# Wide output projections, a position-major first down projection, and the norms' folds moved from GpSimd to VectorE in a two-block layer kernel

## What is computed

```python
x = x + merged @ w_out                      # block 1, output projection, 1024 x 1024
h = rmsnorm(x, norm2_g)
up = causal_dwconv(h @ w_up)                # 1024 x 2816
x = x + (gelu(up) * (h @ w_gate)) @ w_down  # 2816 x 1024: the first down projection
h = rmsnorm_2(x, mix_norm_g)                # block 2
proj = h @ w_in                             # 1024 x 3488
...
x = x + y @ w_out_2                         # block 2, output projection
x = x + (silu(h @ w_gate_2) * (h @ w_up_2)) @ w_down_2
```

## Time and profile before

| | |
|---|---|
| median of 3 runs | 797.68 us (797.62 to 798.31) |
| profiled execution, its own time | 797.33 us |
| its span, first to last instruction | 795.5 us |
| around the span | 1.83 us |
| TensorE matmul busy | 787.8 us, 99% |
| VectorE busy | 582.8 us, 73% |
| ScalarE busy | 453.3 us, 57% |
| GpSimd busy | 75.0 us, 9% |
| mean granted TensorE clock | 0.999 |

### The profile page before, as it was taken

How to read it: one execution, slowest core, us unless ns; L and a number is a source line. 1 busy time by engine, 2 the same in 40 slices (tenths; PEclk the granted TensorE clock), 3 DMA queues, 4 the chain that set the end, 5 groups by cost and what they waited for, 6 DMA issues and landing times.

```text
span 795.5 us, 12020 instructions
## 1 busy us (share of the span) xinstructions
PE 787.8 (99%) x4622; PEld 690.9 (87%) x4622; DVE 582.8 (73%) x705; ACT 453.3 (57%) x594; POOL 75.0 (9%) x92
## 2 busy tenths in 40 slices
PE   8999999999999999999999999999999999999997
PEld 8998888888889899999999897888799888888886
DVE  7986897566577898777787877766878766666664
ACT  7679765666345654544454658767455544454444
POOL 2220231000002000000000532410003000000000
PEclk9999999999999999999999999999999999999999
DMA  8645555443545454555454552444345545455521
GB/s 322 243 161 203 183 192 213 158 159 133 184 159 210 156 205 171 178 194 208 163 206 158 183 197 87 156 159 150 139 155 213 196 181 185 184 198 176 206 105 53
DMA packets 21718, 140.88 MB, mean 177 GB/s; under 512 B 3378, under 2 KB 3506, under 8 KB 5682
## 3 DMA queue, kind: packets, MB, share of 16 engines
q1 hardware_dynamic: 21538, 140.13, 48.9%
q10 hardware_dynamic: 144, 0.26, 0.1%
HBM read 139.33 MB, written 1.05 MB: 176 GB/s over the span
## 4 chain that ended last, share of the span: by engine, by line
PE 97%; DVE 1%; ACT 1%; DMA 1%; issue 0%; SPq 0%; DVEq 0%
PE pp L1577 21%; PE pp L1540 20%; PE pp L1542 20%; PE pp L1541 20%; PE pp L1579 10%; PE pp L1695 1%; PE pp L1721 1%; PE pp L1708 1%; DMA first<-in_first 1%; PE pp L1684 1%; DVE wlo L1051 1%; PE pp L1758 0%; PE pp L1630 0%; PE pp L1642 0%; PE pp L1658 0%; PE pp L1650 0%
## 5 line engine op out<-in xcount | busy, mean ns | idle before, releaser
L950 DVE TENSOR_TENSOR wlo<-raw,whi 128x2048 fp32r<-128x2048 f32 x129 | 298.2, 2314 | 96.2 <-ACT whi L525 95.9
L525 ACT ACTIVATE whi<-raw 128x2048 fp32r<-128x2048 f32 x129 | 246.4, 1911 | 101.2 <-PE pp L1542 101.1
L1577 PE MATMUL pp<-ahilo,whi 128*128 128x512 f32 x704 | 221.4, 396 | 0.0
L1540 PE MATMUL pp<-whi,ahi 128*128 128x512 f32 (+2 forms) x412 | 162.8, 395 | 0.0
L1542 PE MATMUL pp<-whi,alo 128*128 128x512 f32 (+2 forms) x412 | 159.4, 387 | 0.0
L1579 PEld LDWEIGHTS pp<-ahilo,wlo 128*128 128x128 f32 x704 | 132.2, 188 | 31.2
L1541 PE MATMUL pp<-wlo,ahi 128*128 128x512 f32 (+2 forms) x412 | 159.2, 386 | 0.0
L1579 PE MATMUL pp<-ahilo,wlo 128*128 128x256 f32 x704 | 138.3, 278 | 0.0
L1540 PE MATMUL pp<-ahi,whi 128*128 128x256 f32 x416 | 118.5, 285 | 1.4 <-DVE wlo L1051 1.4
L1542 PE MATMUL pp<-ahi,wlo 128*128 128x256 f32 x416 | 117.7, 283 | 0.0
L1541 PE MATMUL pp<-alo,whi 128*128 128x256 f32 x416 | 117.7, 283 | 0.0
(11 more groups left out here) (238 smaller groups left out, 780.7 us busy)
## 6 DMA issues: line engine op xcount, KB each, us to landing
raw<-in_slabs SPq DMA_DIRECT2D x125, 1024.0 KB, 4.8
first<-in_first SPq DMA_DIRECT2D x3, 768.0 KB, 6.9
raw<-in_slabs SPq DMA_DIRECT2D x2, 832.0 KB, 4.4
raw<-in_slabs SPq DMA_DIRECT2D x2, 576.0 KB, 3.7
raw<-in_slabs SPq DMA_DIRECT2D x2, 512.0 KB, 9.9
out<-gg SPq DMA_DIRECT2D x3, 256.0 KB, 2.1
xa<-in_final_norm_g SPq DMA_DIRECT2D x1, 512.0 KB, 6.5
first<-in_first SPq DMA_DIRECT2D x1, 480.0 KB, 3.5
```

The lines of the kernel that those rows point to most:

```text
L525: e.activation(whi[slot][:, :], raw[slot][:, :], ACT.Copy).then_inc(hi_ready, 1)
L950: e.tensor_tensor(wlo[slot][:, :], raw[slot][:, :], whi[slot][:, :].bitcast(f32), ALU.subtract).then_inc(lo_ready, 1)
L1540: e.matmul(out, lhs[0], rhs[0], start=first, stop=False, skip_group_check=True)
L1577: e.matmul(out[:, m, :], w[m][0], ACT2[:, k, :], start=k == 0, stop=False, skip_group_check=True)
```

## The change

1. **Output projections wide.** Both use `feature_pairs` on a buffer `ACT0` that holds high and low side by side, into pairs of banks (2 and 3, or 0 and 1, in turn). `residual` becomes two VectorE instructions, one for each half of the pair.
2. **First down projection position-major**, as the second is: 24 matmuls of 512 columns per slab. X is not added in PSUM: at the end ScalarE copies the four banks to SBUF (`rows`), TensorE transposes them back, 16 in all, in two rounds of 8 (`rows_turn`), and VectorE adds the transposed banks to X (`add_rows`). The first round stands inside the last down slab, the second inside block 2's first strip, before its chunk 2.
3. **Folds on VectorE**, in all four norms, at written places of VectorE's program. `sums(2)` takes two tiles for each half instead of one.
4. `WARM` goes from 11 to 10.

```diff
-WARM = 11
+WARM = 10
...
+        elif out_slab(s) is not None:
+            b = ((3, 1) if s < FFN1 else (1, 3))[out_slab(s) % 2]
...
@@ ScalarE, after FFN 1
-            norm_hi(2, pcol[:, MIXG:MIXG + KD], pairs[0][0], range(KD))
-            for i in range(4):
-                squares(2, i)
+            def rows(c, h):
+                e.wait_ge(down_bank, 2 * c + h + 1)
+                e.activation(outp[:, h, 512 * c:512 * c + 512], ps[2 + 2 * h + c][:, :], ACT.Copy).then_inc(rows_out, 1)
+            rows(0, 0)
+            rows(0, 1)
+            norm_hi(2, pcol[:, MIXG:MIXG + KD], pairs[0][0], (0, 1))
+            rows(1, 0)
+            rows(1, 1)
+            norm_hi(2, pcol[:, MIXG:MIXG + KD], pairs[0][0], (2, 3))
             pre(S2_SEQ + 2)
+            squares(2, 0)
+            squares(2, 1)
+            norm_hi(2, pcol[:, MIXG:MIXG + KD], pairs[0][0], range(4, KD))
+            squares(2, 2)
+            squares(2, 3)
...
@@ VectorE
+            def fold(n, i):
+                e.wait_ge(sq_ready, 4 * n + i + 1)
+                ins = e.tensor_tensor(SQ[:, 0:2, :], SQ[:, 0:2, :], SQ[:, 2 * i:2 * i + 2, :], ALU.add)
+                if i == 3 and n in (0, 2):
+                    ins.then_inc(sq_fold, 1)
+                    return
+                link(ins)
+                if i == 3:
+                    e.tensor_tensor(SQ[:, 0, :], SQ[:, 0, :], SQ[:, 1, :], ALU.add).then_inc(sq_fold, 1)
...
                 lo_part(2, cols, raw[2][:, cols], KD - 2, i == 1)
+            for i in range(1, 4):
+                fold(0, i)
             e.wait_ge(pool_small, 1)
...
-                e.scalar_tensor_tensor(X[:, 2 * i:2 * i + 2, :], ps[BANK[g]][:, :].rearrange("p (m n) -> p m n", m=2),
-                                       0.5, X[:, 2 * i:2 * i + 2, :], ALU.mult, ALU.add).then_inc(bank_free["dve"], 1)
+                x = X[:, 2 * i:2 * i + 2, :]
+                link(e.scalar_tensor_tensor(x, out_pair(s)[:, :, 0:SEQ], 0.5, x, ALU.mult, ALU.add))
+                e.scalar_tensor_tensor(x, out_pair(s)[:, :, SEQ:2 * SEQ], 0.5, x, ALU.mult, ALU.add).then_inc(
+                    bank_free["dve"], 1)
...
                     norm_lo(1, pcol[:, G2:G2 + KD], pairs[2][1], pairs[2][0], (2 * i, 2 * i + 1))
+                    if i > 1:
+                        fold(1, i - 1)
...
                 if s == FFN1 - 1:
+                    fold(1, 3)
                     pre(s + 3)
...
-            for b in range(4):
-                e.wait_ge(down_bank, b + 1)
-                e.tensor_tensor(X[:, 2 * b:2 * b + 2, :], ps[2 + b][:, :].rearrange("p (m n) -> p m n", m=2),
+            def add_rows(b):
+                e.wait_ge(rows_T, b + 1)
+                e.tensor_tensor(X[:, 2 * b:2 * b + 2, :], PSX[b][:, :].rearrange("p (m n) -> p m n", m=2),
                                 X[:, 2 * b:2 * b + 2, :], ALU.add).then_inc(x_ready, 1)
-                if b:
-                    norm_lo(2, pcol[:, MIXG:MIXG + KD], pairs[0][1], pairs[0][0], (2 * b - 2, 2 * b - 1))
-            norm_lo(2, pcol[:, MIXG:MIXG + KD], pairs[0][1], pairs[0][0], (6, 7))
-            pre(S2_SEQ + 1)
-            pre(S2_SEQ + 2)
+            for c in range(2):
+                add_rows(2 * c)
+                add_rows(2 * c + 1)
+                norm_lo(2, pcol[:, MIXG:MIXG + KD], pairs[0][1], pairs[0][0], range(4 * c, 4 * c + 4))
+                pre(S2_SEQ + 1 + c)
+            for i in range(1, 4):
+                fold(2, i)
...
@@ TensorE
+            def rows_turn(c):
+                e.wait_ge(rows_out, 2 * c + 2)
+                for m in range(4):
+                    for h in range(HALVES):
+                        o = SEQ * (m % 2) + P * h
+                        ins = e.transpose(PSX[2 * c + m // 2][:, o:o + P],
+                                          outp[:, h, 512 * c + P * m:512 * c + P * m + P], ident[:, :])
+                    if m % 2:
+                        ins.then_inc(rows_T, 1)
...
+                    for a in range(2):
+                        for i in range(4):
+                            if last and which == 1:
+                                c, h, k = a, i // 2, i % 2
...
+                                        weights(slot, k, slice(512 * c, 512 * c + 512), D), first and k == 0, False,
+                                        (lambda: rows_turn(0)) if last and which == 1 and (a, i) == (1, 1) else None)
...
-                    S2_SEQ: lambda k: e.wait_ge(h_lo, 2 * KD + k + 1),
+                    S2_SEQ: lambda k: (rows_turn(1) if k == 2 else None, e.wait_ge(h_lo, 2 * KD + k + 1)),
+                    S2_SEQ + 1: lambda k: e.wait_ge(h_lo, 2 * KD + k + 1),
```

More of the change, by code:

```diff
@@ L106, in half_strip, with out_slab @@
     return None
+def out_slab(s):
+    if S_OUT <= s < FFN1:
+        return s - S_OUT
+    return s - S2_OUT if S2_OUT <= s < FFN2 else None
 def gate_strip(s):
@@ L253, in program @@
         X, T0, T1 = (chunks[:, :, SEQ * i:SEQ * i + SEQ] for i in range(3))
-        ACT2 = sb("ahilo2", [P, KD, 2 * SEQ], f32r)
-        pairs = [(sb("ahi0", [P, KD, SEQ], f32r), sb("alo0", [P, KD, SEQ], f32r)),
+        ACT0, ACT2 = (sb(f"ahilo{i}", [P, KD, 2 * SEQ], f32r) for i in (0, 2))
+        pairs = [(ACT0[:, :, 0:SEQ], ACT0[:, :, SEQ:2 * SEQ]),
                  (sb("ahi1", [P, KD, SEQ], f32r), sb("alo1", [P, KD, SEQ], f32r)),
@@ L347, in program, with out_pair @@
         PSM = (ps[6], ps[7], ps[4], ps[5])
+        def out_pair(s):
+            return pp[((1, 0) if s < FFN1 else (0, 1))[out_slab(s) % 2]]
         def gate_half(c, h):
@@ L369, in program @@
         PSPV2 = ps[5][:, SEQ:2 * SEQ]
+        PSX = (ps[0], ps[1], ps[2], ps[3])
         PSCQ = (ps[3], ps[4], ps[3])
@@ L1419, in _ @@
                     norm_lo(3, pcol[:, FFNG:FFNG + KD], pairs[2][1], pairs[2][0], (2 * i, 2 * i + 1))
+                    if i > 1:
+                        fold(3, i - 1)
                 if s == FFN2 - 1:
+                    fold(3, 3)
                     pre(s + 3)
@@ L1448, in _ @@
         def _(e):
[L1449 to L1459, removed]
-                    e.tensor_tensor(SQ[:, 0, :], SQ[:, 0, :], SQ[:, 1, :], ALU.add).then_inc(sq_fold, 1)
             e.wait_ge(first_in[0], 16)
@@ L1465, in _ @@
             e.tensor_scalar(sp[:, 2, :], pcol[:, LAM:LAM + KD], -1.0, None, ALU.mult).then_inc(pool_small, 1)
-            fold(0)
             for s in range(S_XR, S_G):
@@ L1478, in _ @@
                                 ALU.subtract).then_inc(ya_lo, 1)
-            fold(1)
-            fold(2)
             steps = [0]
@@ L1532, in _, with three @@
                            ropeB[:, 0, h, :], ropeB[:, 1, h, :], 4, 16, mla_ready if i and h else None)
-            fold(3)
         @block.tensor
         def _(e):
-            def three(out, lhs, rhs, first, last):
+            def three(out, lhs, rhs, first, last, between=None):
                 e.matmul(out, lhs[0], rhs[0], start=first, stop=False, skip_group_check=True)
+                if between:
+                    between()
                 e.matmul(out, lhs[0], rhs[1], start=False, stop=False, skip_group_check=True)
@@ L1569, in feature_tiles, with feature_pairs @@
                 return ins
-            def feature_pairs(out, slot, ready):
+            def feature_pairs(out, slot, ready, act=ACT2):
                 for k in range(KD):
@@ L1576, in feature_pairs @@
                     for m in range(2):
-                        e.matmul(out[:, m, :], w[m][0], ACT2[:, k, :], start=k == 0, stop=False, skip_group_check=True)
+                        e.matmul(out[:, m, :], w[m][0], act[:, k, :], start=k == 0, stop=False, skip_group_check=True)
                     for m in range(2):
-                        ins = e.matmul(out[:, m, 0:SEQ], w[m][1], ACT2[:, k, 0:SEQ], start=False, stop=k == KD - 1,
+                        ins = e.matmul(out[:, m, 0:SEQ], w[m][1], act[:, k, 0:SEQ], start=False, stop=k == KD - 1,
                                        skip_group_check=True)
@@ L1611, in sums @@
                     for h in range(HALVES):
-                        ins = e.matmul(sums_bank(n)[:, h:h + 1], SQ[:, 0, P * h:P * h + P], ones[:, 0:1], start=True,
-                                       stop=True, skip_group_check=True)
+                        for i in range(2):
+                            ins = e.matmul(sums_bank(n)[:, h:h + 1], SQ[:, i, P * h:P * h + P], ones[:, 0:1],
+                                           start=(h, i) == (0, 0), stop=(h, i) == (1, 1), skip_group_check=True)
                 else:
@@ L1825, in slab @@
                                         (act[0][:, blk, :], act[1][:, blk, :]), m == 0, True)
+                    elif out_slab(s) is not None:
+                        ins = feature_pairs(out_pair(s), slot, at, ACT0)
                     elif layout == "feature" and kind == "cols":
@@ L1914, in down @@
                     acthi, actlo = act_parts[last]
[L1915 to L1932 removed]
+                    for a in range(2):
```

(13 more changed lines are left out.)

20 lines of the change are left out of this document (2 added, 18 removed).

## The result

The changed kernel takes **793.39 us**, median of 5 runs (793.37 to 793.64), against 797.68 for the kernel before in the same rounds (797.55 to 798.31): a ratio of 0.9948 with an interval of 0.9938 to 0.9959. The profiled execution took 793.6 us, with a span of 791.8.

What follows compares the result with a forecast made beforehand. TensorE, busy for 99% of the span, was taken as the bound. The terms -3.53 - 1.33 + 1.75 + 0.30 - 1.43 + 0.29 = -3.95 us gave 793.4, plus 0.35 for the median: 793.7 us, range 792.8 to 795.4.

Steps and rivals of the forecast that it cites:

- Down projection: First FFN's down projection: eleven slabs go from 5.77 to 5.45 us with 24 wide matmuls instead of 48, -3.53 us.
- Output projections: Both output projections: eight slabs go from 5.76 to 5.57 us, one of them gaining nothing, -1.33 us.
- The transposes: From FFN 1 to block 2: sixteen added transposes cost +1.75 us, and TensorE's wait at the first round +0.30 us.
- narrow place of 0.2 us: Block 2's first strip, chunks 0 and 4: VectorE's work was forecast ready only 0.2 us before TensorE needs it.
- Start: Norm 0's folds leave GpSimd: the 1.43 us wait before slab 2 goes, sums at 20.25 instead of 21.68, -1.43 us.
- the sign that I had named for being wrong: At the start: a first pair whose matmuls start 0.24 us apart would show the forecast wrong.
- Sums 2: Sums of norm 2: four products take 0.92 us where TensorE lost 0.63 before, +0.29 us.
- In the middle of the kernel nothing waited for that: Away from the start, nothing waited for GpSimd's slow additions or the VectorE work they slowed; no gain priced there.
- the gate at the start stays: Rival: GpSimd does not cause VectorE's long instructions, so slab 2 at the start still waits; 795.5 us, chance 0.08.
- block 2's first strip waits: Rival: the path to chunk 4 falls behind by one low part and TensorE waits 2.1 us; 795.8 us, chance 0.10.
- Cost by columns: Rival: matmul cost goes with columns, not the number of matmuls, so wide forms save nothing; 798.6 us, chance 0.02.
- VectorE as the bound in the output projections: Rival: in the eight output slabs the second residual instruction is paid in full, 5.84 us; 799.6 us, chance 0.03.

## Why the prediction was right, step by step

**Down projection**, -3.53 us: right. The pass of 16.59 us was reached, and the split of the second down projection shows that the number of matmuls is the reason.

**Output projections**, 0.19 a slab and none from block 2's slab 0: right. The stretches gave 0.70 and 0.59 for 0.76 and 0.57, and the wait before block 2's slab 1 is there with 0.29 us. Undone, the wide form cost 1.28 in these two stretches.

**The transposes**: right in sum, +1.07 and -2.40 for +1.17 and -2.36, but not by its own step. I had TensorE wait 0.26 us for ScalarE's copies. It didn't: the matmul before started at 434.78 and the transposes at 435.01, the usual 0.23, for ScalarE's copies were done at 433.90 + 1.06 = 434.96. ScalarE's timeline:

```profile
433.90 1.06 ACT L842 ACTIVATE gg<-pp 128x512 f32<-128x512 f32 x2
```

The same time went elsewhere: the last down slab began at 431.25 and block 2 at 437.80, 6.55 us for 5.45 + 0.87 = 6.32. Its first matmul stands 431.56 - 431.25 = 0.31 us before the next, and so does the first one behind the transposes (435.87 to 436.18), where 0.227 is the usual: 0.17 in all. The other 22 are 0.230 apart, 0.07 in all. The one behind the transposes was in the forecast, the one at the slab's start was not. The forecast had the slab's input there "with 0.1 to spare". VectorE made it until 430.42 + 0.69 = 431.11, but TensorE loads it as weights ahead of the matmul: that load started at 431.22, 0.23 us after the load before had ended, where the down slab that starts at 409.22 has its load at 409.11 without a gap. I read this as a short wait for VectorE, which is not shown: the profile names no releaser. Eight transposes cost 435.87 - 435.01 = 0.86 and 441.33 - 440.54 = 0.79 us, as priced. Neither narrow place of 0.2 us opened: behind the last down slab the matmuls follow each other without a gap.

**Start**, -1.43 us: right, but only for an execution whose first matmuls are fast. All three stretched instructions and the 1.43 us wait fell with GpSimd's additions. Counted from the moment at which ScalarE takes up the input, the start went from 15.21 to 13.77 us, 1.44 less. The path was as forecast too: VectorE's second half is ready 10.87 us after that moment (16.99 + 1.22 - 7.34), which from 7.15 makes 18.02 for my 18.0. Two things were missing. The moment itself differs from execution to execution, by 0.3 us in the profiles, and the kernel before's profile had caught an early one; that is 0.19 of the 0.34 by which the profiled 1.09 falls short. And I took the first pair as free of the warm-ups, but in the profiled execution its first four matmuls were 0.24 us apart, the sign that I had named for being wrong. So TensorE reached the sums at 20.59, after the folds' end at 20.27; that is the other 0.16. The medians of both kernels give 1.23 and 1.24, over executions of both sorts.

**Sums 2**: four products for two, 0.92 us forecast and 453.13 - 452.32 = 0.81 measured, and no wait for the folds (they end at 449.37). With the distance ahead of them it makes 453.13 - 452.10 - 0.23 = 0.80 for 0.63 before: +0.17 for the +0.29 of the sum.

**"In the middle of the kernel nothing waited for that"**: true of the kernel before, not of this one. With wide slabs GpSimd's last additions come 0.22 us late at sums 1 and 3. The number was not hurt, as the change moves them, but I had priced at nothing what is worth 0.66 us together with the wide slabs.

**The rivals.** That the gate at the start stays fell with both kernels that move norm 0's folds. That block 2's first strip waits fell with the 15.33 us stretch. Cost by columns fell with the split. VectorE as the bound in the output projections fell: the slabs are 5.58 us apart, no distance between TensorE's matmuls in them stands out but that before block 2's slab 1, and VectorE waits 0.47 or 0.48 us for TensorE before three of the eight residuals.

**The time itself.** The sum was -3.95 us. The profiled spans gave -3.7 and the medians -4.29, so the forecast of 793.7 lies 0.3 above the median and, without the 0.35 that it adds for the median of the runs, 793.4 would lie 0.2 below the profiled 793.6. The 0.35 was the scatter of three runs of the kernel before: in the later groups its median is 797.36 to 797.51, 0.03 to 0.18 above the 797.33 of its profile. That the forecast comes within 0.3 us is in part luck, as these differences are as large as the ones between the terms.

## What to carry to other kernels

When one engine fills the span, price each form by the distance between the starts of its instructions in the trace: the same columns in half the matmuls saved 0.32 us a slab here. Work on an idle engine is free only if it doesn't slow a neighbour: GpSimd's additions held up nobody themselves, and cost 1.2 to 1.4 us through VectorE. When a stretch becomes shorter, look again at everything that used to end just ahead of its end. To compare two kernels to a tenth, compare stretches between marks of their traces, and look first at when the input came in each.

## What I had not expected of the hardware

- While GpSimd adds, VectorE's instructions take 0.48 + 0.74 = 1.22 and 0.69 + 1.09 = 1.78 us, the same in two kernels to the hundredth; I had expected some slowing, not one that repeats so exactly. The same shows at norm 1: a low part of 2048 columns that began 0.36 us before the end of GpSimd's last addition took 2.50 us, where it takes 2.29 when VectorE adds.
- A 256-column f32 addition takes GpSimd 0.74 us and VectorE 0.42, a 512-column one 1.30 and about 0.7.
- The first four real matmuls start 0.14 us apart on average in some executions of the kernel after and 0.24 in others, after the same warm-ups. The one is near the 0.12 us of the rest, the other twice that, as it would be at the lower of TensorE's two levels (1.2 and 2.4 GHz). But the granted clock that the profile gives for 0 to 8 us is 1.00 in both, so no row shows the lower level, and this reading rests on the distances alone.
- The folds' end follows the arrival of one piece of the input to 0.02 us in twelve profiles, through some 13 us of work on ScalarE and VectorE; the arrival itself varies by 0.3 us.
